# One fp32 transformer pair on one core: all riding modulation summed on VectorE, query statistics inside units, rstd spread by a broadcast stationary, and a slab's last tiles handled one by one

## The chip, the cores and the metric

The kernel runs on one core of one Trainium2 chip. The metric is the device time of one execution in microseconds (us). TensorE is PE here, VectorE DVE, ScalarE ACT, GpSimd POOL, and SyncE, which issues most of the transfers, SP.

## What is computed

Two transformer blocks run one after the other over 256 tokens of width 1024 (with 256 context tokens beside them in the first part). All matrices are fp32.

```python
# first block, S = 256 tokens, D = 1024
ml = split(silu(c) @ w_mod + b_mod, 9)            # the modulation: 9 chunks of 1024, for tokens and for context
x = x + 0.5 * ml[2] * swiglu(modulate(rms_norm(x), ml[0], ml[1]))    # "ffn1", inner width 2816; the context too
...                                                # w_in, 8 query heads, attention, convolution, gates, "merge", "wout"
x = x + 0.5 * ml[8] * swiglu(modulate(rms_norm(x), ml[6], ml[7]))    # "ffn2"
x = rms_norm(x, final_g)
# second block
h = rms_norm_2(x, norm_mix)                        # then its own attention, pooling and "wout2"
x = x + square(relu(rms_norm_2(x, norm_mlp) @ w_ff1)) @ w_ff2        # "ff", inner width 4096
return rms_norm_2(x, norm_final)
```

## The kernel before

All five engines run programs written by hand, tied by semaphores. Features lie on the 128 partitions and tokens in the columns, so an activation of width 1024 is 8 tiles (`KD`).

**Units.** The weights are cut into 161 units of 1 MB (eight 128-row blocks by 256 columns; some have six blocks). SP loads unit k into `raw[k % 2]`. ACT rounds it into `w_hi` (L510, `split`), in two halves; DVE takes the rest into `w_lo` (L945, its own `split`); PE multiplies in three products, high by high, low by high and high by low (L1702 to L1704; where both activations lie side by side, L1699 does the first two in one matmul of 512 columns). PE then adds to `halves_done`, the result is taken out of PSUM `ps_u`, and `drained` counts that. SP may load unit k + 2 once both halves of `w_lo` of unit k are made. Each engine's queue is in program order, so where a `split` stands decides what waits behind it.

**ffn1** is three slabs of inner tiles (8, 8 and 6 units), each followed by 4 output units (`out_step`), 34 units in all. Beside it ride the modulation's weights: 36 loads of 1 MB, a quarter of a chunk each. The first 8 (`MOD_FRONT`) are multiplied on PE before ffn1 (`front_mod`, L1662), with dummy matmuls between them (`keep_busy_front`, L1764). Of the other 28 (`MOD_RIDE`), 20 (`MOD_SUMMED`) are multiplied and summed on DVE during ffn1, four instructions a quarter (`mod_products`, L977 and L980), and after four quarters PE sums the partitions (`mod_sum`, L1678, 16 instructions in the trace) and DVE turns the chunk into columns (`modulation`, L989). The last 8 quarters go through PE (`late`, L1662): one in ffn1, seven around the norm behind it.

**A norm** between stages goes like this. DVE adds an output unit onto the pair of tiles of `x` (`add_out`, L1062). ACT squares both (`squares`, L555). POOL adds the squares of tiles 0 to 5 into tile 0 as they come. PE sums over partitions, 128 tokens a matmul of one column (`stat`, L1640: tiles 6, 7 and the sum). ACT takes the root (L539), DVE the reciprocal (L1010) and four diagonal matrices out of it (L1013, two for 256 tokens), PE multiplies these by ones, which spreads the value over the partitions (`spread`, L1646), and DVE scales each tile (L1024), ACT rounds it (L547), DVE makes the rest (L1033), and PE's next unit takes tile by tile. `keep_busy` (L1651) fills PE with dummy matmuls meanwhile.

**Queries** come as 4 units q0 to q3. Each head's squares are summed over partitions by `q_stat`, four matmuls a unit (L1834): three units' worth stand behind q3 and the fourth behind the first gates unit.

**ff** has four slabs of 4 inner units (8 tiles) and 4 output units. Of an inner unit ACT copies half of the result (L597), DVE adds the other half (L1070), takes relu and the row factor (L1604), ACT squares (L899) and rounds (L901), and DVE makes the rest (L1608), each time for both tiles of the unit in one instruction of 512 columns. The output unit needs tiles 6 and 7 last.

## Time and profile before

| what | value |
|---|---|
| median of 3 runs | 1279.79 us (1277.67, 1279.79 and 1280.79) |
| the profiled execution | 1281.16 us |
| its span, first to last instruction | 1279.4 us |
| PE busy | 1253.2 us, 98% |
| DVE busy | 850.3 us, 66% |
| ACT busy | 588.9 us, 46% |
| DMA | 214.22 MB, mean 167 GB/s |
| mean granted clock of PE | 0.993 |

The profiled execution took 1.76 us beyond its span and lay 1.37 us above the median. A time in the sections below is counted from the start of the span. One fp32 matmul shows as two records, so that 12 matmuls of `stat` are 24 records.

### The profile page before, as it was taken

To read this page: it belongs to the slowest core of one execution; us is meant where nothing else is said; L and a number is where in the kernel's file an instruction comes from. 1 tells how busy PE (TensorE), PEld (TensorE's weight loads), DVE (VectorE), ACT (ScalarE), POOL (GpSimd) and SP (SyncE) were. 2 spreads that over 40 slices of the span, in tenths; PEclk is the share of its full clock that TensorE was granted. 3 is DMA by queue.
4 is the path that set the end of the run, shared out by engine and by line. 5 is a ranking of instruction groups with operands and counts; after the bars stand their busy time and mean duration, and the time that the engine had idled before them with its cause. 6 is when DMAs were issued, how large, how long until landed. Compare 5 with 4: busy or idle time off the path is not lost.

```text
span 1279.4 us, 20913 instructions
## 1 busy us (share of the span) xinstructions
PE 1253.2 (98%) x7854; PEld 1097.3 (86%) x7854; DVE 850.3 (66%) x1356; ACT 588.9 (46%) x878; POOL 53.3 (4%) x65
## 2 busy tenths in 40 slices
PE   8999999999999999999999999999999999999997
PEld 6788888888887899888999888888899999888886
DVE  3677777763344755777666676666769977666765
ACT  3543234321233336644435654546465565554552
POOL 2000000000002000100001000000001301000001
PEclk8999999999999989999999999999999999999999
DMA  9655544444224334423445555554533334455442
GB/s 376 262 197 197 198 180 170 180 193 164 91 75 165 132 132 137 159 98 105 160 169 173 217 197 180 189 190 146 218 132 120 111 132 169 161 190 201 166 169 95
DMA packets 30962, 214.22 MB, mean 167 GB/s; under 512 B 3376, under 2 KB 4656, under 8 KB 5936
## 3 DMA queue, kind: packets, MB, share of 16 engines
q1 hardware_dynamic: 30320, 211.83, 45.9%
q10 hardware_dynamic: 576, 1.48, 0.3%
q8 instruction: 46, 0.75, 0.2%
q14 instruction: 20, 0.16, 0.0%
HBM read 212.24 MB, written 1.05 MB: 167 GB/s over the span
## 4 chain that ended last, share of the span: by engine, by line
PE 85%; DVE 6%; DMA 4%; ACT 3%; issue 1%; DVEq 0%; SPq 0%; ACTq 0%
PE ps_u L1704 25%; PE ps_u L1702 18%; PE ps_u L1703 18%; PE ps_u L1699 15%; DMA raw<-in_stream 2%; DVE w_lo L945 2%; PE ps_a L1628 1%; PE ps_a L1662 1%; PE ps_a L1881 1%; DMA wide_scr<-in_mods 1%; DMA scr<-in_mods 1%; PE ps_a L1866 1%; ACT w_hi L510 1%; PE ps_a L2065 1%; DVE sq L1024 1%
## 5 line engine op out<-in xcount | busy, mean ns | idle before, releaser
L945 DVE TENSOR_TENSOR w_lo<-raw,w_hi 128x1024 fp32r<-128x1024 f32 x322 | 393.4, 1224 | 148.4 <-ACT w_hi L510 147.3
L510 ACT ACTIVATE w_hi<-raw 128x1024 fp32r<-128x1024 f32 x322 | 339.1, 1056 | 323.2 <-PE ps_u L1704 222.5
L1704 PE MATMUL ps_u<-x_hi,w_lo 128*128 128x256 f32 (+1 forms) x1488 | 462.1, 311 | 0.0
L1702 PE MATMUL ps_u<-x_hi,w_hi 128*128 128x256 f32 (+1 forms) x1136 | 370.6, 326 | 2.2 <-DVE x_lo L1033 1.9
L1703 PE MATMUL ps_u<-x_lo,w_hi 128*128 128x256 f32 (+1 forms) x1072 | 345.2, 322 | 0.0
L1704 PEld LDWEIGHTS ps_u<-x_hi,w_lo 128*128 128x128 f32 x1488 | 283.8, 191 | 15.1
L1704 PE MATMUL ps_u<-h_hi,w_lo 128*128 128x256 f32 (+1 forms) x800 | 244.0, 305 | 0.0
L1702 PEld LDWEIGHTS ps_u<-x_hi,w_hi 128*128 128x128 f32 x1136 | 217.5, 191 | 21.1 <-issue 5.2
L1703 PEld LDWEIGHTS ps_u<-x_lo,w_hi 128*128 128x128 f32 x1072 | 205.3, 191 | 16.0 <-issue 0.7
L1704 PEld LDWEIGHTS ps_u<-h_hi,w_lo 128*128 128x128 f32 x800 | 151.6, 189 | 6.9
L1702 PE MATMUL ps_u<-h_hi,w_hi 128*128 128x256 f32 (+1 forms) x432 | 141.9, 328 | 0.8 <-DVE x L1062 0.4
L1699 PE MATMUL ps_u<-h_hi,w_hi 128*128 128x512 f32 x368 | 130.5, 399 | 3.2 <-DVE h_hi L1608 3.2
L1699 PE MATMUL ps_u<-x_hi,w_hi 128*128 128x512 f32 x352 | 125.0, 400 | 0.2 <-DVE x_hi L1033 0.2
L1703 PE MATMUL ps_u<-h_lo,w_hi 128*128 128x256 f32 (+1 forms) x368 | 122.9, 334 | 0.0
L1699 PE MATMUL ps_u<-x_lo,w_hi 128*128 128x512 f32 x256 | 90.4, 398 | 0.7 <-DVE h_hi L1608 0.7
L1702 PEld LDWEIGHTS ps_u<-h_hi,w_hi 128*128 128x128 f32 x432 | 82.1, 190 | 9.4 <-issue 1.2
L1699 PEld LDWEIGHTS ps_u<-h_hi,w_hi 128*128 128x128 f32 x368 | 69.1, 188 | 21.5 <-DVE h_hi L1608 3.9
L1699 PEld LDWEIGHTS ps_u<-x_hi,w_hi 128*128 128x128 f32 x352 | 66.1, 188 | 17.6 <-issue 0.8
L1703 PEld LDWEIGHTS ps_u<-h_lo,w_hi 128*128 128x128 f32 x368 | 69.9, 190 | 6.9
L1704 PE MATMUL ps_u<-x_lo,w_lo 128*128 128x256 f32 x256 | 71.5, 279 | 0.0
L1070 DVE TENSOR_TENSOR s<-ps_u,s 128x512 f32<-128x512 f32 x38 | 26.3, 692 | 52.8 <-ACT s L597 52.3
L1699 PEld LDWEIGHTS ps_u<-x_lo,w_hi 128*128 128x128 f32 x256 | 48.1, 188 | 12.4 <-DVE h_hi L1608 1.0
(277 smaller groups left out, 1215.6 us busy)
## 6 DMA issues: line engine op xcount, KB each, us to landing
raw<-in_stream SPq DMA_DIRECT2D x153, 1024.0 KB, 4.8
wide_scr<-in_mods SPq DMA_DIRECT2D x18, 1024.0 KB, 7.1
scr<-in_mods SPq DMA_DIRECT2D x18, 1024.0 KB, 6.9
raw<-in_stream SPq DMA_DIRECT2D x8, 768.0 KB, 4.2
x<-in_tokens SPq DMA_DIRECT2D x2, 1024.0 KB, 6.6
wide_scr<-in_cmp_w SPq DMA_DIRECT2D x2, 1024.0 KB, 7.8
sq<-in_cmp_w SPq DMA_DIRECT2D x2, 1024.0 KB, 7.5
out<-x SPq DMA_DIRECT2D x4, 256.0 KB, 2.2
```

The costliest lines, as they stand in the source:

```text
L510: act.activation(w_hi[:, k % 2, cols], raw[:, k % 2, cols], ACT.Copy).then_inc(h_ready, 1)
L945: dve.tensor_tensor(w_lo[:, k % 2, cols], raw[:, k % 2, cols], w_hi[:, k % 2, cols].bitcast(F32), ALU.subtract).then_inc(l_ready, 1)
L1024: ins = dve.scalar_tensor_tensor(sq[:, kc, cols], x[:, kc, cols], scale(kc, s), ps_a[:, 2, spread_cols], ALU.mult, ALU.mult)
L1070: dve.tensor_tensor(both, ps_u[:, b:b + 2, 0:S], both, ALU.add).then_inc(halves_summed, 1)
L1628: return pe.transpose(dst, src, ident[0:n, 0:n])
L1662: ins = pe.matmul(ps_a[rows, b, 0:MOD_COLS], sc_pad[:, 2 * quarter + kc, :], mod_slots[slot][:, lo:lo + MOD_COLS], start=(quarter == 0 and ...
L1699: pe.matmul(ps_u[:, 2 * b + t, :], wh, both, start=(kc == 0), stop=False)
L1702: pe.matmul(dst, wh, xh, start=(kc == 0), stop=False)
L1703: pe.matmul(dst, wh, xl, start=False, stop=False)
L1704: ins = pe.matmul(dst, wl, xh, start=False, stop=(kc == span - 1))
L1866: ins = pe.matmul(ps_a[:, qt, :], q_cur[:, j, qt * P:(qt + 1) * P], k_all[:, g, :], start=True, stop=True)
L1881: ins = pe.matmul(ps_a[:, 2, 0:S], v_tok[:, c, g, :], probs_t[:, c, :], start=(c == 0), stop=(c == 3))
```

## The change

The eight quarters that went through PE are multiplied on DVE as the twenty before them (`MOD_SUMMED` is 28), so all 28 riding loads are issued within ffn1, and PE gets two more `mod_sum`. What DVE and ACT did after ffn1 for the second block's gate weights (`wg_hi`, `wg_lo`) moves into it. `keep_busy_front` starts with 31 dummies instead of 22. `q_stat` is called within the units q2, q3 and the first two gates units. `spread` no longer takes diagonals: the stationary operand is the reciprocal itself, broadcast along the columns, and the identity is streamed, 128 columns a matmul. In three norms `stat` is cut into the sum's part and the part of tiles 6 and 7, with dummies between. A new semaphore, `first_added`, lets ACT start on the first tile of a pair. At the norms two halves of `split` move ahead of `add_out`, one behind `norm_lo`. And in ff the last inner unit of a slab goes tile by tile.

```diff
 MOD_RIDE = N_MOD * MOD_QUARTERS - MOD_FRONT
-MOD_SUMMED = 5 * MOD_QUARTERS
...
-MOD_BANKS = (0, 1, 2, 0, 1)
+MOD_BANKS = (0, 1, 2, 0, 1, 2, 0)
...
                     sp.wait_ge(mod_done, MOD_FRONT + n - 3)
-                elif n < MOD_SUMMED + 4:
+                else:
                     sp.wait_ge(mod_added, 4 * (n - 3))
-                else:
-                    sp.wait_ge(mod_done, MOD_FRONT + n - MOD_SUMMED - 3)
                 mod_load(MOD_FRONT + n, n % 4)
 
...
-                if n <= MOD_RIDE - 4:
-                    riding_load(n)
+                riding_load(n)
...
             units(FIRST["k"], 2)
-            for n in range(MOD_RIDE - 3, MOD_RIDE):
-                riding_load(n)
             run(FIRST["k"] + 2, FIRST["ffn2"])
...
+                    if t == 0 and early is not None:
+                        act.wait_ge(first_added, early)
+                    else:
+                        act.wait_ge(drained, 2 * pr + (k + 3))
                     act.activation(sq[:, m + t, 0:n], x[:, m + t, 0:n], ACT.Square).then_inc(sq_ready, 1)
...
                 if last and i == 3:
                     squares(pr, k0 + 2, 4, n)
-                    squares(pr, k0 + 3, 6, n)
+                    if more:
+                        split(pr, k0 + 5, 0)
+                    squares(pr, k0 + 3, 6, n, early)
...
                 dve.wait_ge(root_done, n + 1)
                 dve.reciprocal(rstd[:, 0:tiles], root[:, 0:tiles]).then_inc(recip_done, 1)
-                dve.wait_ge(recip_done, n + 1)
-                for t in range(tiles):
-                    ins = dve.tensor_scalar(t1[:, 0, t * P:(t + 1) * P], ident, rstd[:, t:t + 1], None, ALU.mult)
-                ins.then_inc(diag_done, 1)
...
+                    if first and t == 0:
+                        ins.then_inc(first_added, 1)
                 ins.then_inc(drained, 1)
...
                 hurry = last and more and i >= 2
-                if more and not (hurry and i == 3):
+                if hurry and i == 3:
+                    split(pr, k0 + i + 1, 1)
+                if more:
                     split(pr, k0 + i + 2, 0)
                 if made is not None:
                     add_halves(pr, k0 + i, 2 * i, gate, made + i)
                 else:
-                    add_out(pr, k0 + i, 2 * i, n, gate)
-                if hurry and i == 3:
-                    split(pr, k0 + i + 1, 1)
+                    add_out(pr, k0 + i, 2 * i, n, gate, first=last and i == 3)
                 if more and not hurry:
                     split(pr, k0 + i + 2, 1)
 
...
+
+            dve.memset(sq_gain[:, :, 0], 1.0)
+            dve.tensor_tensor(sq_gain[:, :, 1], vec[:, V_F1:V_F1 + KD], vec[:, V_F1:V_F1 + KD], ALU.mult)
...
+                                if c == 5:
+                                    scale_of(2, 7, V_N3)
+                                if c == 6:
+                                    gates_of(1, 8)
+                            if at + u == MOD_SUMMED:
+                                dve.wait_ge(wg_done, 1)
+                                dve.tensor_tensor(wg_lo[:], wg, wg_hi[:].bitcast(F32), ALU.subtract).then_inc(wg_ready, 1)
...
             swiglu(FIRST["ffn1"], 0, NB, 0)
-            dve.wait_ge(wg_done, 1)
-            dve.tensor_tensor(wg_lo[:], wg, wg_hi[:].bitcast(F32), ALU.subtract).then_inc(wg_ready, 1)
-            split(0, FIRST["k"] + 1, 0)
             spread(1, 4)
-            split(0, FIRST["k"] + 1, 1)
             dve.wait_ge(scale_ready, 2)
             norm_lo(1, 1, NB, modulated(1, 4), 3)
-            modulation(7, 7, 0)
-            scale_of(2, 7, V_N3)
-            modulation(8, 8, 1)
-            gates_of(1, 8)
+            split(0, FIRST["k"] + 1, 1)
...
-            split(0, FIRST["ffn2"] + 1, 0)
             spread(2, 2)
+            norm_lo(2, 2, S, modulated(2, 7), 6, beside=True)
             split(0, FIRST["ffn2"] + 1, 1)
-            norm_lo(2, 2, S, modulated(2, 7), 6, beside=True)
             swiglu(FIRST["ffn2"], 22, S, 1)
...
+                    if u < 3:
+                        two = slice(2 * u, 2 * u + 2)
                         dve.scalar_tensor_tensor(both, both, 0.0, r_both, ALU.max, ALU.mult).then_inc(relu_done, 1)
...
+                    else:
+                        for t in range(2):
+                            dve.scalar_tensor_tensor(both[:, t, :], both[:, t, :], 0.0, r_ff, ALU.max, ALU.mult).then_inc(relu_done, 1)
+                        split(pr, k + u + 2, 0)
+                        for t in range(2):
+                            m = 2 * u + t
+                            dve.wait_ge(hh_done, c + m - u + 1)
+                            ins = dve.tensor_tensor(h_hi[:, m, S:NB], t1[:, j, t * S:(t + 1) * S], h_hi[:, m, 0:S].bitcast(F32), ALU.subtract)
+                            ins.then_inc(drained if t else last_lo, 1)
+                    split(pr, k + u + 2, 1)
...
+            def stat(n, tiles):
+                stat_rows(n, tiles, (*range(SUMMED, KD), 0), SUMMED, 0)
+
+            def stat_sums(n, tiles):
+                stat_rows(n, tiles, (0,), 0, KD - 1)
+
+            def stat_rest(n, tiles):
+                stat_rows(n, tiles, range(SUMMED, KD), 0, KD - 1)
...
             def spread(n, tiles):
-                pe.wait_ge(diag_done, n + 1)
-                pe.matmul(ps_a[:, 2, 0:tiles * P], ones[:], t1[:, 0, 0:tiles * P], start=True, stop=True).then_inc(rb_done, 1)
+                pe.wait_ge(recip_done, n + 1)
+                for t in range(tiles):
+                    ins = pe.matmul(ps_a[:, 2, t * P:(t + 1) * P], rstd[:, t:t + 1].broadcast_to([P, P]), ident, start=True, stop=True)
+                ins.then_inc(rb_done, 1)
...
-            def late(n):
-                u = MOD_FRONT + n
-                c = u // MOD_QUARTERS
-                mod(u, 1 if c == N_MOD - 1 else 0, u % MOD_QUARTERS, n % 4, LANDED * (n // 4 + 3), c - 1)
...
                             c, behind = divmod(k + o - 1, MOD_QUARTERS)
                             if behind == MOD_QUARTERS - 1 and c < MOD_SUMMED // MOD_QUARTERS:
                                 mod_sum(c)
-                            if k + o == MOD_SUMMED + 2:
-                                late(MOD_SUMMED)
...
-            keep_busy_front(22)
+            keep_busy_front(31)
...
-            late_units = iter(range(MOD_SUMMED + 1, MOD_RIDE))
-            for n in itertools.islice(late_units, 3):
-                late(n)
-            stat(1, 4)
-            for n in itertools.islice(late_units, 2):
-                late(n)
+            pe.wait_ge(cst_landed, 16)
+            pe.wait_ge(mod_turned, N_MOD)
+            stat_sums(1, 4)
+            keep_busy(3)
+            stat_rest(1, 4)
+            keep_busy(2)
             spread(1, 4)
-            for n in late_units:
-                late(n)
+            keep_busy(4)
...
+            unit(0, kq + 3, from_x(S), ready=stat_within(1))
 
             pe.wait_ge(k_ready, 2)
...
-            gates(0, 0)
-            q_stat(3)
-            gates(0, 1)
+            gates(0, 0, stat_within(2))
+            gates(0, 1, stat_within(3))
...
-            keep_busy(3)
-            stat(2, 2)
+            stat_sums(2, 2)
+            keep_busy(2)
+            stat_rest(2, 2)
             keep_busy(2)
             spread(2, 2)
-            keep_busy(4)
+            keep_busy(3)
...
+            def hidden_ready(pr, k, slab):
+                def ready(kc):
+                    if kc == 6:
+                        pe.wait_ge(last_lo, slab + 1)
+                    else:
+                        pe.wait_ge(drained, 2 * pr + (k + kc // 2 + 3))
+                return ready
...
+            stat_sums(5, 2)
             keep_busy(2)
-            stat(5, 2)
+            stat_rest(5, 2)
             keep_busy(2)
             spread(5, 2)
```

PE where ffn1 ends, before: output units (L1704), late quarters (L1662), statistics (L1640), the spread (L1646), then the first unit of w_in.

```order
L1704 MATMUL ps_u<-h_hi,w_lo 128x512
L1662 MATMUL ps_a<-wide_scr,sc_pad 32x256 x8
L1662 MATMUL ps_a<-scr,sc_pad 32x256 x16
L1640 MATMUL ps_a<-ones,sq 128x1 x12
L1662 MATMUL ps_a<-wide_scr,sc_pad 32x256 x16
L1646 MATMUL ps_a<-t,ones 128x512
L1662 MATMUL ps_a<-scr,sc_pad 32x256 x16
```

The same place with the change (statistics L1658, spread L1675, dummies L1681):

```order
L1658 MATMUL ps_a<-ones,sq 128x1 x4
L1681 MATMUL ps_a<-cst,ones 128x256 x3
L1658 MATMUL ps_a<-ones,sq 128x1 x8
L1681 MATMUL ps_a<-cst,ones 128x256 x2
L1675 MATMUL ps_a<-cst,rstd 128x128 x4
L1681 MATMUL ps_a<-cst,ones 128x256 x4
```

The seven late quarters are gone, the sum's part of the statistics stands first, and dummies stand where the quarters stood.

DVE at the same place, before: the last addition (L1062), weight remainders (L945), gate weights (L1190), reciprocal, diagonals, and the first tiles of the norm.

```order
L1062 SCALAR_TENSOR_TENSOR x<-ps_u,gate_half,x 128x256 x8
L945 TENSOR_TENSOR w_lo<-raw,w_hi 128x1024
L1190 TENSOR_TENSOR wg_lo<-late_w,wg_hi 128x192
L945 TENSOR_TENSOR w_lo<-raw,w_hi 128x1024
L1010 RECIPROCAL rstd<-root 128x4
L1013 TENSOR_SCALAR t<-cst,rstd 128x128 x4
L945 TENSOR_TENSOR w_lo<-raw,w_hi 128x1024
L1024 SCALAR_TENSOR_TENSOR sq<-x,am,ps_a 128x256 x4
L1033 SCALAR_TENSOR_TENSOR x_lo<-sq,mods,x_hi 128x256 x2
```

With the change (L1066 is the addition, L955 the remainders, L1018 the reciprocal, L1028 and L1037 the norm):

```order
L1066 SCALAR_TENSOR_TENSOR x<-ps_u,gate_half,x 128x256 x4
L955 TENSOR_TENSOR w_lo<-raw,w_hi 128x1024 x2
L1066 SCALAR_TENSOR_TENSOR x<-ps_u,gate_half,x 128x256 x4
L1018 RECIPROCAL rstd<-root 128x4
L1028 SCALAR_TENSOR_TENSOR sq<-x,am,ps_a 128x256 x4
L1037 SCALAR_TENSOR_TENSOR x_lo<-sq,mods,x_hi 128x256 x2
```

Nothing stands any more between the last addition, the reciprocal and the norm.

DVE at the last inner unit of an ff slab, with the change; before, the row of L1621 was one instruction of 512 columns, and so was that of L1626.

```order
L1076 TENSOR_TENSOR s<-ps_u,s 128x512
L1621 SCALAR_TENSOR_TENSOR s<-s,q_cur 128x256 x2
L955 TENSOR_TENSOR w_lo<-raw,w_hi 128x1024
L1626 TENSOR_TENSOR h_hi<-t,h_hi 128x256 x2
L955 TENSOR_TENSOR w_lo<-raw,w_hi 128x1024 x2
```

The weight half stays between the relu and the remainder, as before.

## Rows read from the trace of the kernel before

**Rows 1.** The page's busy part: us (share of the span) xinstructions.

```profile
PE 1253.2 (98%) x7854; PEld 1097.3 (86%) x7854; DVE 850.3 (66%) x1356; ACT 588.9 (46%) x878; POOL 53.3 (4%) x65
```

**Rows 2.** Waits of PE: waiting line <- releaser: us in total, times, longest.

```profile
PE ps_u L1699 <- DVE h_hi L1608: 3.9, 6, 0.8
PE ps_a L1662 <- DMA wide_scr<-in_mods: 2.9, 1, 2.9
...
PE ps_a L1646 <- DVE t L1013: 1.4, 2, 0.7
...
PE ps_a L1932 <- DVE x_lo L1107: 0.4, 1, 0.4
```

**Rows 3.** Timeline of the front: start us, us, engine, line, tiles, [idle before].

```profile
24.54 1.16 PE L1764 MATMUL ps_u<-ones 128*128 128x128 f32 x8
...
25.58 6.36 DVE L1024 SCALAR_TENSOR_TENSOR sq<-x,am,ps_a 128x256 f32<-128x256 f32 x16
...
32.37 1.07 PE L1662 MATMUL ps_a<-scr,sc_pad 128*32 128x256 f32 x16 [0.41 <-DMA scr<-in_mods]
...
34.12 0.44 DVE L989 STREAM_TRANSPOSE turned<-ps_a 128x256 f32<-128x256 f32 x1
```

**Rows 4.** Two `mod_sum` on PE's timeline, four ffn1 units apart.

```profile
47.94 1.07 PE L1678 MATMUL ps_a<-sq,one_col 128*32 128x256 f32 x16
...
92.72 1.07 PE L1678 MATMUL ps_a<-sq,one_col 128*32 128x256 f32 x16
```

**Rows 5.** Groups by line and form: xcount | busy us, mean ns of one | idle before.

```profile
L980 DVE SCALAR_TENSOR_TENSOR sq<-scr,sc_pad,sq 128x1024 f32<-128x1024 f32 x40 | 48.7, 1278 | 0.0
...
L1145 DVE TENSOR_TENSOR h_hi<-t,h_hi 128x256 f32 x22 | 9.4, 425 | 14.7 <-ACT h_hi L627 14.7
```

**Rows 6.** Timeline where ffn1 ends.

```profile
405.07 1.66 DVE L1062 SCALAR_TENSOR_TENSOR x<-ps_u,gate_half,x 128x256 f32<-128x256 f32 x4 [6.50 <-PE ps_u L1704]
...
407.69 2.84 PE L1640 MATMUL ps_a<-ones,sq 128*128 128x1 f32 x24
...
411.08 0.87 DVE L1013 TENSOR_SCALAR t<-cst,rstd 128x128 f32<-128x128 f32 x4
...
413.71 1.65 DVE L1024 SCALAR_TENSOR_TENSOR sq<-x,am,ps_a 128x256 f32<-128x256 f32 x4 [0.63 <-PE ps_a L1646]
...
426.07 0.88 DVE L1033 SCALAR_TENSOR_TENSOR x_lo<-sq,mods,x_hi 128x256 fp32r<-128x256 f32 x2 [0.19 <-ACT x_hi L547]
```

**Rows 7.** Query statistics on PE's timeline.

```profile
468.14 3.08 PE L1834 MATMUL ps_a<-ones,scr 128*128 128x1 f32 x24
```

**Rows 8.** Windows: stretch, length, busy (x started) of PE, PEld, DVE, ACT, POOL; clock, DMA share, GB/s.

```profile
463.00:467.00 4.00, 4.00 (x36) 4.00 (x35) 3.80 (x8) 1.06 (x1) 0.00 (x0) 1.00 0.33 96
470.00:478.00 8.00, 8.00 (x43) 8.00 (x44) 2.10 (x3) 1.39 (x3) 0.00 (x0) 0.57 0.41 133
```

**Rows 9.** Timeline between wout and ffn2.

```profile
701.65 1.11 PE L1651 MATMUL ps_a<-cst,ones 128*128 128x256 f32 x4
703.47 0.70 PE L1646 MATMUL ps_a<-t,ones 128*128 128x256 f32 x2 [0.70 <-DVE t L1013]
...
704.46 0.86 DVE L1024 SCALAR_TENSOR_TENSOR sq<-x,am,ps_a 128x256 f32<-128x256 f32 x2
```

**Rows 10.** Timeline of the first ff slab's last inner unit, and PE's wait in the last slab.

```profile
1109.51 0.69 DVE L1604 SCALAR_TENSOR_TENSOR s<-s,q_cur 128x512 f32<-128x512 f32 x1
...
1111.88 0.69 DVE L1608 TENSOR_TENSOR h_hi<-t,h_hi 128x512 f32 x1 [0.54 <-ACT h_hi L901]
...
1112.63 0.49 PE L1699 MATMUL ps_u<-h_hi,w_hi 128*128 128x512 f32 x1 [0.68 <-DVE h_hi L1608]
...
1250.21 0.51 PE L1699 MATMUL ps_u<-h_hi,w_hi 128*128 128x512 f32 x1 [0.63 <-DVE h_hi L1608]
```

**Rows 11.** Timeline of the final norm.

```profile
1270.25 1.50 PE L1640 MATMUL ps_a<-ones,sq 128*128 128x1 f32 x12 [0.43 <-ACT sq L555]
...
1273.56 3.22 DVE L1621 SCALAR_TENSOR_TENSOR x<-x,vec,ps_a 128x256 f32<-128x256 f32 x8 [0.79 <-PE ps_a L1646]
```

More of the change, by code:

```diff
@@ L1051, in plain, with add_out @@
                 return lambda kc, s: vcol(v, kc)
-            def add_out(pr, k, m, n, gate, b=None):
+            def add_out(pr, k, m, n, gate, b=None, first=False):
                 done(pr, k)
@@ L1100, in out_parts @@
             def out_parts(n, k, m, gate, dst, hi, gain):
-                add_out(0, k, m, S, gate)
+                add_out(0, k, m, S, gate, first=True)
                 if m < KD - 2:
@@ L1628, in turn, with stat_rows @@
                 return pe.transpose(dst, src, ident[0:n, 0:n])
-            def stat(n, tiles):
+            def stat_rows(n, tiles, rows, first, last):
                 made = n if n < 3 else n - 1
-                for kc in (*range(SUMMED, KD), 0):
+                for kc in rows:
                     if kc == 0:
@@ L1812, in turn_v, with q_stat, stat_within @@
                 ins.then_inc(v_turned, 1)
+            def q_stat(i):
+                pe.wait_ge(q_squared, 2 * i + 2)
+                for h in range(2 * i, 2 * i + 2):
+                    for t in range(TT):
+                        at = 16 + TT * h + t
+                        ins = pe.matmul(ps_a[:, 1, at:at + 1], q_sq[:, h, t * P:(t + 1) * P], ones[:, 0:1], start=True, stop=True)
+                ins.then_inc(qstat_done, 1)
+            def stat_within(i):
+                return lambda kc: q_stat(i) if kc == 4 else None
             kq = FIRST["q"]
```

126 lines of the change are left out of this document (62 added, 64 removed).

## The prediction, written before the changed kernel ran

> **What bounds the kernel now.** I read the page first: PE is busy 98% of the span, so the time is PE's queue, and only two things can shorten it: work taken off PE, and stretches in which it idles, runs dummies, or runs at the low clock [rows 1]. Then PE's waits, to see who holds it: the three that this change touches are the remainder of the last ff tiles (3.9 us in six waits), the diagonals of the spread (1.4 in two) and one tile of `x_lo` (0.4) [rows 2]. Waits alone miss what dummies and late quarters cover, so I read the timeline at each norm, and last the windows, for the clock. There the reader sees a stretch behind the query statistics at a mean granted clock of 0.57.
>
> **Front.** PE waits 2.9 us for the first quarter [rows 2], and 31 dummies instead of 22 fill that. What ends the front is another chain: DVE scales tiles from 25.58 for 6.36 us, makes two weight halves (2.35 us) and turns the second chunk at 34.12, while PE waited for the last quarter's load until 32.37 and then multiplied for 1.07, to 33.44 [rows 3]. The loads don't come sooner for a faster PE, as they queue behind each other. So at most 34.12 - 33.44 = 0.7 us is to be had, if DVE's scaling starts sooner (no diagonals, a warm PE). The spread by four matmuls of 128 columns costs 1.16 us (eight records [rows 3]). I take **0.6 us gained**, bounds 0 and 0.7.
>
> **ffn1.** PE loses one late quarter and gets two `mod_sum`, 1.07 us each, as each quarter is also 1.07 [rows 3, 4]. Net **1.1 us lost**. DVE gets 8 quarters of four instructions at 1.28 us, about 5.1 us a unit [rows 5]. Two sums are 44.8 us apart, that is four units of 10.9 and the sum [rows 4]; DVE's other work in such a unit (two weight halves of some 1.2 us, two products or four additions, 1.66 [rows 6]) leaves about 2 us of it free, as it did for the 20 units before, in which PE has no wait for DVE [rows 2]. So DVE's share costs nothing; without that slack it would cost PE up to 5 us a unit.
>
> **Where ffn1 ends.** PE's last output unit is over at about 405.0 (DVE adds from 405.07). Before, three quarters run first, the statistics take 407.69 to 410.5, 24 records of 0.116 us, then quarters, the diagonals from 411.08 for 0.87, and the scaling starts at 413.71, 3.25 us behind the statistics [rows 6]. With the change: the sum's part, 8 records, 0.93 us, to 405.9; three dummies, six records at some 0.25 (four take 1.11 [rows 9]), 1.5 us, to 407.4; tiles 6 and 7, 16 records, 1.86 us, to 409.3, whose squares are there by then (added by 406.73 [rows 6]). Two dummies, 1.1 us, cover root and reciprocal; the spread takes 1.16 and DVE starts some 0.2 later: 411.7. That is **2.0 us gained**, as the first w_in unit goes at the norm's pace to its last tile, at 426.95 before [rows 6]. The half `split` that now stands behind the norm is needed only halfway through the next unit; the next load waits on it and comes later than before, two units ahead of its use. The transposes that followed the norm are gone, but PE had the next unit's weights. Unknown is the broadcast stationary operand: no row shows one. From below it costs nothing more than the dummies' load. From above I let each of eight weight loads stand uncovered for 0.1 us, 0.8 in all. I take the low end, as dummies whose operand changes nothing in kind run at 0.145 a record [rows 3]. Bounds 1.2 and 2.4.
>
> **Query statistics.** 24 records take 3.08 us behind q3 [rows 7]. In the 8 us from 470 the clock granted is 0.57 of full, the lower of its two levels (1.2 GHz) for most of it, and 43 matmuls start; at the full clock (2.4 GHz) 36 start in 4 us [rows 8]. 43 would take 4.8 us: 3.2 us are lost. What PE did before the fall is that string of matmuls of one column. With the change no more than 8 records stand together. The matmuls themselves stay. I take **3.0 us gained**, bounds 0 and 3.4 (half of 8 x 0.86).
>
> The Trainium skill bears on that (TensorE: Matmul & The Clock Gate, Part 1): the gate halves the clock by how busy PE has lately been, it does not start afresh with a kernel, so where it falls varies from run to run. The trace has the fall at this place, in full. By the rule some runs of before may not have the fall at all, and then the sum gains nothing here; that is a rival below.
>
> **Between wout and ffn2.** The dummies behind the statistics start at 701.65, the scaling at 704.46, 2.8 us later, with PE's wait of 0.70 for the diagonals and a weight half in DVE's queue between [rows 9]. With the change two dummies (1.1), two spread matmuls (0.6, half of 1.16) and 0.2: 1.9, so 0.9 gained. The sum's part, 4 records or 0.45 us, goes ahead. **1.3 us gained**, bounds 0.7 and 1.6. The load that a moved half releases comes later, and the two loads of compression weights with it; the one is two units ahead of its use, the others are for the second block.
>
> **Into the second block.** The wait of 0.7 for the diagonals (half of 1.4) and that of 0.4 for `x_lo` go [rows 2]: the reciprocal is there when PE is, and ACT rounds tile 6 while DVE adds tile 7, one addition earlier (0.4, a quarter of 1.66 [rows 6]). **1.1 us gained**, bounds 0.4 and 1.1.
>
> **ff.** In each of four slabs PE waits at tile 6 of the first output unit, from 0.68 in the first to 0.63 in the last; the sum over the four is 2.6 of the 3.9 [rows 2, 10] (two other waits, in the first slab, stay: they hang on units that the change leaves whole). The relu starts at 1109.51, the remainder of both tiles at 1111.88 and PE at 1112.63 [rows 10]. One by one: an instruction of 256 columns takes 0.425 against 0.69 [rows 5, 10], so both relus end some 0.1 later than one did, the weight half behind them too (0.6 from start to start for the relu, 0.1 more, 1.2 for the half), at about 1111.45. ACT has by then squared and rounded tile 6. Its remainder then ends at 1111.9, and PE starts at 1112.0, when it is ready anyway (1112.63 - 0.68 = 1111.95). 0.6 of each wait goes, and no more than the wait: **2.4 us gained**, bounds 1.0 and 2.6. Tile 7 follows 0.4 later, under PE's matmuls of tile 6.
>
> The skill has a rule against this step (VectorE: DVE Perf Modes, The TRN2 errata): each instruction pays a fixed latency, so tiles of at least 512 elements are the better ones. The rows bear the rule out: 2 x 0.425 is 0.16 more than 0.69 [rows 5, 10]. By the rule DVE and ACT lose a little in each slab; by the rows the first tile still comes sooner, and neither engine ends the slab.
>
> **End.** The statistics shrink by the sum's 0.45 us, while root, dummies and spread take 1.9 as before (from about 1271.7 to 1273.56 [rows 11]). **0.4 us gained**, bounds 0.2 and 0.9.
>
> **Sum.** 0.6 - 1.1 + 2.0 + 3.0 + 1.3 + 1.1 + 2.4 + 0.4 = 9.7 us. Against the profiled execution of 1281.16 us that is 1271.5. It lies 1.37 above the median of before, 1279.79, from which the sum gives 1270.1. Either could be the better base, as the runs spread by 3.5 us; I take **1270.8 us**.
>
> **Rivals.**
> *The clock falls elsewhere, or fell in few runs before* (0.20). For it: the runs shown spread from 1277.67 to 1280.79, about the size of one fall. Against: the profiled run has it in full. Then 6.7 us are gained, 1273.1 from the median, or 1274.5 from the profile.
> *The slabs of ff keep their wait* (0.08): ACT's queue is what is late, as its weight half stands ahead of the copy. Without the 2.4: 1273.2.
> *More is gained* (0.05): the front is freed more than the loads seem to allow, by the 2.9 us of the first wait, 1268.
> *DVE falls behind in ffn1* (0.04). This one ends on the other side. In the 8 units that newly carry quarters a weight half would come late and PE wait. For it: 5.1 us more a unit. Against: 20 units of the same kind show none. It decides from 1.7 us a unit on: 8 x 1.7 = 13.6 us, time 1284.7.
> *The gain is given back* (0.05): each norm starts sooner and the next unit waits for its weights or loads instead, so that only q and ff remain at half size: 1277.
> The forecast has 0.58, and its own range is 1268 to 1273.5.
>
> A measurement of this kernel tells about 0.3%, 3.8 us, from no change, so faster means under 1276.0. Forecast, clock, ff and the larger gain lie there, 0.91, of which I give 0.03 to the zone between for bounds that add up badly: faster 0.88, same 0.08, slower 0.04. The range reaches from all upper bounds that are likely together, 1267, to past the clock rival, 1276: it leaves out about 2 in 10.
>
> **What the profile after would show.** No low clock around 470, and the same number of q statistics in four pieces. Statistics where ffn1 ends over at about 4.3 us behind the last unit, scaling at 6.7 (8.7 before). No wait for L1013, which is gone. The waits of L1699 for the remainder at about 1.3 us in total instead of 3.9. Two sums more in ffn1, and no PE wait on DVE there. The prediction is wrong if the clock falls at another place, if the broadcast operand makes a spread matmul longer than 0.3 us, or if waits on weight halves appear behind the norms.

## The result, and the profile after

The changed kernel took 1265.93 us, the median of four runs (1263.96 to 1267.28), against 1278.73 for the kernel before in runs on the same chip (four, 1276.84 to 1280.79): a ratio of 0.9894, 95% interval 0.9873 to 0.9915. The profiled run took 1267.28, its span 1265.5. Between the two profiled spans lie 13.9 us; I had worked out 9.7, and the time of 1265.9 is under my range of 1267 to 1276. Taken a second time, among the experiments, it had 1265.84 us (0.9892, 0.9866 to 0.9917).

The page's busy part and span, with the columns of [rows 1]:

```profile
span 1265.5 us, 20715 instructions
...
PE 1247.6 (99%) x7814; PEld 1098.2 (87%) x7814; DVE 883.0 (70%) x1378; ACT 589.2 (47%) x886; POOL 54.5 (4%) x65
```

PE's busy time fell by only 5.6 us where the span fell by 13.9: most of the gain is waits. PE's waits, as [rows 2] shows them for before:

```profile
PE ps_a L1692 <- DMA scr<-in_mods: 2.2, 1, 2.2
PE ps_u L1727 <- DVE x_lo L1037: 1.9, 2, 1.3
PE ps_a L2087 <- DVE q_cur L1519: 1.7, 2, 1.1
...
PE ps_u L1724 <- DVE h_hi L1154: 0.7, 1, 0.7
```

The top row of before, six waits of 3.9 us for the remainder of the ff tiles, has gone altogether (I had left 1.3 of it), and so have the diagonals. One row of those shown is new, the last: 0.7 us of wait in ffn2.

To see where the 13.9 us lie I cut both profiled executions at the same PE instructions (times between the starts of these, in us):

| stage, ended by | before | after | gained | forecast |
|---|---|---|---|---|
| front, first `mod_sum` | 47.94 | 48.45 | -0.5 | +0.6 |
| ffn1 and its norm, key statistics | 391.94 | 390.19 | +1.8 | -1.1 + 2.0 |
| k, v, q units, first swap of the gates | 39.72 | 36.68 | +3.0 | +3.0 |
| attention, wout, behind wout's last unit | 219.11 | 219.09 | 0.0 | 0 |
| norm, first unit of ffn2 | 7.43 | 5.40 | +2.0 | +1.3 |
| ffn2 | 190.79 | 190.41 | +0.4 | 0 |
| norm, first stage of the second block | 18.92 | 17.34 | +1.6 | +1.1 |
| second block, statistics ahead of ff | 171.55 | 171.55 | 0.0 | 0 |
| ff | 181.40 | 176.86 | +4.5 | +2.4 |
| final norm, end of the span | 10.59 | 9.53 | +1.1 | +0.4 |

The largest miss is ff, 2.1 us of the 4.2 by which the sum was short. The table compares one profile of each kernel. Some stages of the old code vary between its profiles: ff took 180.3 to 184.1 us in five of them (176.9 to 177.5 in three of the new), the stage into the second block 18.6 to 18.9 in seven (17.3 in all of the new).

In the first slab's last inner unit of after, what answers to [rows 10] reads, in order of time, with one row of ACT (it squares the two tiles) among those of DVE:

```profile
1099.01 0.68 DVE L1076 TENSOR_TENSOR s<-ps_u,s 128x512 f32<-128x512 f32 x1
1099.72 0.76 DVE L1621 SCALAR_TENSOR_TENSOR s<-s,q_cur 128x256 f32<-128x256 f32 x2
...
1100.18 0.76 ACT L909 ACTIVATE t<-s 128x256 f32<-128x256 f32 x2 [0.33 <-DVE s L1621]
1100.40 1.22 DVE L955 TENSOR_TENSOR w_lo<-raw,w_hi 128x1024 fp32r<-128x1024 f32 x1
...
1101.54 0.75 DVE L1626 TENSOR_TENSOR h_hi<-t,h_hi 128x256 fp32r<-128x256 f32 x2
```

From the start of the relu to the start of the first remainder it takes 1.8 us; before it took 1109.51 to 1111.88, 2.4. PE multiplies all the while.

Where ffn1 ends, against [rows 6]:

```profile
406.65 0.94 PE L1658 MATMUL ps_a<-ones,sq 128*128 128x1 f32 x8
...
408.84 1.84 PE L1658 MATMUL ps_a<-ones,sq 128*128 128x1 f32 x16
...
411.01 0.18 DVE L1018 RECIPROCAL rstd<-root 128x4 f32<-128x4 f32 x1 [2.50 <-ACT root L535]
...
411.49 1.05 PE L1675 MATMUL ps_a<-cst,rstd 128*128 128x128 f32 x8
...
412.65 1.66 DVE L1028 SCALAR_TENSOR_TENSOR sq<-x,am,ps_a 128x256 f32<-128x256 f32 x4 [1.46 <-PE ps_a L1675]
```

The scaling starts 6.0 us behind PE's last output unit; 8.7 before, 6.7 forecast. The broadcast operand costs nothing: 8 records in 1.05 us, where 8 of a dummy with the same 128 columns took 1.16 [rows 3].

The clock at the query statistics, and in the front (windows as in [rows 8]):

```profile
457.00:479.00 22.00, 22.00 (x185) 21.79 (x183) 12.99 (x20) 9.40 (x14) 0.00 (x0) 1.00 0.39 139
```

```profile
32.00:36.00 4.00, 3.37 (x24) 2.10 (x25) 1.91 (x4) 0.68 (x2) 0.00 (x0) 0.57 0.69 223
```

The fall near 470 is gone (1.00 throughout), but in the front there is one at 32 to 36, a granted clock of 0.57, on the very chain that ends the front.

### The profile page after: what moved, and what is told of

It reads as the page before. It is cut to its first block, busy times and chain, and to the rows that moved or that the text cites. A ratio compares the mean times of both kernels' runs of the same rounds, so it can differ in the third digit from the quotient of the medians.

```text
span 1265.5 us, 20715 instructions
## 1 busy us (share of the span) xinstructions
PE 1247.6 (99%) x7814; PEld 1098.2 (87%) x7814; DVE 883.0 (70%) x1378; ACT 589.2 (47%) x886; POOL 54.5 (4%) x65
## 3 DMA queue, kind: packets, MB, share of 16 engines
HBM read 212.24 MB, written 1.05 MB: 169 GB/s over the span
## 4 chain that ended last, share of the span: by engine, by line
PE 92%; DVE 3%; DMA 2%; ACT 1%; issue 1%; SPq 0%; DVEq 0%; ACTq 0%
PE ps_u L1729 27%; PE ps_u L1727 19%; PE ps_u L1728 19%; PE ps_u L1724 17%; PE ps_a L1646 1%; DMA wide_scr<-in_mods 1%; DVE w_lo L955 1%; PE ps_a L1902 1%; DMA scr<-in_mods 1%; PE ps_a L1887 1%; PE ps_a L1658 1%; PE ps_a L1703 1%; PE ps_a L2087 1%; DMA raw<-in_stream 1%; PE ps_a L1681 0%
## 5 line engine op out<-in xcount | busy, mean ns | idle before, releaser
L955 DVE TENSOR_TENSOR w_lo<-raw,w_hi 128x1024 fp32r<-128x1024 f32 x322 | 393.3, 1223 | 120.0 <-ACT w_hi L506 119.0
L1728 PEld LDWEIGHTS ps_u<-x_lo,w_hi 128*128 128x128 f32 x1072 | 204.0, 190 | 15.5 <-issue 0.5
L988 DVE SCALAR_TENSOR_TENSOR sq<-scr,sc_pad,sq 128x1024 f32<-128x1024 f32 x56 | 68.1, 1279 | 0.0
```

The source lines that it names most:

```text
L955: dve.tensor_tensor(w_lo[:, k % 2, cols], raw[:, k % 2, cols], w_hi[:, k % 2, cols].bitcast(F32), ALU.subtract).then_inc(l_ready, 1)
L988: ins = dve.scalar_tensor_tensor(total_v, w[:, kc, :], by, total_v, ALU.mult, ALU.add)
L1728: pe.matmul(dst, wh, xl, start=False, stop=False)
```

## Experiments

In the tables, **time beyond pace** is summed over PE's matmuls of one stage: what each start-to-start distance has over 237 ns (512 columns) or 120 ns (256), where it is over by more than 15%.

### The inner units of ff written out, the tiles still in pairs

The diff also turned the `Fori` loop over the inner units, which computes its addresses in registers, into straight code; I had priced only the tiles that go singly. This kernel is the one before with this alone, on ACT and DVE:

```diff
-                with dve.Fori(0, 2) as p:
-                    for j in range(2):
-                        sum_halves(k + j, j, c - 22 + 2 * p + (j + 1))
+                for u in range(4):
+                    j = u % 2
+                    sum_halves(k + u, j, c - 22 + u + 1)
...
-                        two = ds(4 * p + 2 * j, 2)
+                    two = slice(2 * u, 2 * u + 2)
```

> The kernel before with one edit: the inner units of an ff slab are written out one by one on ACT and DVE instead of in a loop of two over register addresses; both tiles of the last one stay together. In the two traces that I have, the ff stage took 178.4 us before and 173.8 after, 4.7 less where I had forecast 2.4. Theory U (the loop's address work was part of each wait): the six waits for the remainder (3.9 us) shrink to under 1.5, the stage takes about 175.7 us (2.7 less: 0.34 from each of four chains and the 1.3 of the first slab), the time is about 1276, ratio 0.998. Theory T (the tiles going singly did it all): the stage stays at 178.4 within 0.4, the time at that of before.

1274.94 us (12 runs) against 1278.76: ratio 0.9971, 0.9956 to 0.9986, that is 3.7 us. The stage ff took 178.51, the waits that were 3.9 us are off the list of PE's waits. Its neighbour, the changed kernel with the last inner unit's tiles in a pair again:

```diff
-                    if u < 3:
+                    if u < 4:
...
-                    if kc == 6:
-                        pe.wait_ge(last_lo, slab + 1)
-                    else:
-                        pe.wait_ge(drained, 2 * pr + (k + kc // 2 + 3))
+                    pe.wait_ge(drained, 2 * pr + (k + kc // 2 + 3))
```

> The changed kernel with one part undone: the last inner unit of a slab is rounded, squared and left with its remainder as a pair of tiles again; the loops stay written out. Theory U: about 0.3 us of wait comes back in each slab but no more, the ff stage takes 175 to 176 us, the time is 1267.5 to 1268.5. Theory T: all waits are back, the stage takes 178.4, the time is 1270.6.

1267.17 us (0.9900, 0.9882 to 0.9918), the stage 178.09. The expectations count ff from the start of its second unit, 3.0 us behind the table's cut; by the table's, theory U expected 178.7 and 178 to 179, and theory T 181.4 for both. U holds; the 3.7 us in the runs are more than the 2.7 that it gave.

### Which engine's loop

The same edit on one engine each, in the kernel before.

> The kernel before with one edit: DVE's inner units of an ff slab are written out, ACT's stay in the loop over register addresses (both tiles of the last one together). PE's time beyond its pace in ff was 4.8, 5.8 and 8.1 us in kernels with both loops and 2.0 with both written out. If DVE's loop is what made the remainder late (theory D), it falls to under 3 here; if ACT's (theory A), it stays over 4; if each adds its share of the address work, both this kernel and its counterpart show 3 to 4. Time by D: 1275.5, by A: 1278 or more.

> The counterpart: ACT's inner units of an ff slab are written out, DVE's stay in the loop. Theory D: PE's time beyond its pace in ff stays over 4 us, the time at 1278 or more. Theory A: it falls to under 3 us, the time to 1275.5. Shares: 3 to 4 us in both.

| kernel | loops on | beyond pace in ff | stage ff | ratio to before |
|---|---|---|---|---|
| before, two profiles | both | 5.8, 5.5 | 181.4, 180.3 | 1 |
| three other kernels with that code | both | 4.8, 8.1, 4.8 | 180.4, 184.1, 181.3 | |
| ACT written out | DVE | 4.3 | 178.9 | 1.0012 (1.0001 to 1.0024) |
| DVE written out | ACT | 2.9 | 178.4 | 0.9982 (0.9965 to 1.0000) |
| both written out | none | 2.0 | 178.5 | 0.9971 (0.9956 to 0.9986) |
| changed, tiles in a pair | none | 1.4 | 178.1 | 0.9900 (0.9882 to 0.9918) |
| changed, two profiles | none | 0.9, 0.6 | 176.9, 177.4 | 0.9894, 0.9892 |

From the start of the relu to the start of the remainder (all 16 units) it takes 2.30 to 2.39 us before, 2.20 to 2.29 with ACT written out, 2.15 to 2.17 with DVE and 2.06 with both; in the changed kernel the first of two single tiles makes it 1.82. The remainder's group, by line and form, tells it directly. Its last figure is DVE's idle time ahead of these 16 instructions. In order: before taken a second time, DVE written out, ACT written out, both:

```profile
L1608 DVE TENSOR_TENSOR h_hi<-t,h_hi 128x512 f32 x16 | 11.1, 692 | 8.7 <-ACT h_hi L901 8.7
```

```profile
L1608 DVE TENSOR_TENSOR h_hi<-t,h_hi 128x512 fp32r<-128x512 f32 x16 | 11.1, 692 | 5.3 <-ACT h_hi L901 5.3
```

```profile
L1608 DVE TENSOR_TENSOR h_hi<-t,h_hi 128x512 f32 x16 | 11.1, 692 | 7.0 <-ACT h_hi L901 7.0
```

```profile
L1608 DVE TENSOR_TENSOR h_hi<-t,h_hi 128x512 fp32r<-128x512 f32 x16 | 11.1, 693 | 3.7 <-ACT h_hi L901 3.7
```

The instruction itself is as long in all four. What shrinks is the pause ahead of it, by 3.4 us through DVE's loop and 1.7 through ACT's (of 8.7): 0.21 and 0.11 us a unit, or 0.3 of a chain that was 0.5 to 0.9 us too long. Most is DVE's, as theory D had it, and the shares of the pause add up. ACT's own share stands in its rows too, as idle time for which the view names no releaser, ahead of the instruction that makes `h_hi`: 2.2 us with the loop (before taken a second time), 0.5 without (ACT written out).

```profile
L901 ACT ACTIVATE h_hi<-t 128x512 f32 x16 | 10.1, 632 | 2.2
```

```profile
L901 ACT ACTIVATE h_hi<-t 128x512 fp32r<-128x512 f32 x16 | 10.1, 633 | 0.5
```

The times add up less well than the pauses: 2.3 us gained by DVE's loop alone (1277.18 us, where theory D expected 1275.5), 3.7 by both, and by ACT's alone no gain, if anything a loss of 1.5 us that no stage of its profile shows (its profiled run was its quickest, 1274.92, with the quick pace in ffn2 of which the last section tells). That PE's wait fell by more than the chain's 0.3 us a slab, and to nothing, is seen but not fully explained: with both loops, single waits in a slab ran from 0.2 to 2.3 us between executions, and what made the long ones stays open.

### The query statistics within units

```diff
+            def stat_within(i):
+                return lambda kc: q_stat(i) if kc == 4 else None
...
-            unit(0, kq + 3, from_x(S))
-            for i in range(3):
-                q_stat(i)
+            unit(0, kq + 3, from_x(S), ready=stat_within(1))
```

> The kernel before with one edit: the query statistics go into units, eight matmuls at a time. Theory C (the string of 24 matmuls of one column is what the clock falls behind): no low clock near 470, the q stage 3.0 us shorter, the time 1275.7. Rival: the fall comes from what was run earlier and only moves; then the low clock stands somewhere within the next 20 us and the time stays within 1 us of before.

1276.76 us (0.9976, 0.9960 to 0.9991). The stage of the query units took 36.68 us against 39.72 and the clock stayed up there, but where ffn1 ends a fall came that the first profile of before didn't have, and cost 1.3 us (393.23 against 391.94):

```profile
409.00:413.00 4.00, 4.00 (x41) 2.98 (x44) 3.02 (x7) 1.63 (x3) 0.00 (x0) 0.75 1.01 424
413.00:417.00 4.00, 4.00 (x46) 1.45 (x38) 1.89 (x5) 0.58 (x2) 0.00 (x0) 0.82 1.02 426
464.00:478.00 14.00, 14.00 (x118) 13.90 (x117) 9.46 (x15) 6.48 (x9) 0.00 (x0) 1.00 0.37 121
```

So was the string of one-column matmuls the cause, or did the fall only move? I broke the string with dummies:

```diff
             for i in range(3):
+                if i:
+                    for _ in range(2):
+                        pe.matmul(ps_a[:, 1, S:2 * S], ones[:], cos1, start=True, stop=True)
                 q_stat(i)
```

> The kernel before with one edit: between the three groups of eight query statistics behind q3 stand two dummies of 256 columns each, 1.0 us a time, 2.0 in all. In all three profiles of kernels with the plain string of 24 the clock falls within 3 us of its start, for 3.4 or 6.8 us, and in none of the three without. Theory C (a long stretch of one-column matmuls is behind the fall): no low clock from 465 to 480, and the q stage takes 36.7 + 2.0 = 38.7 us. Rival (something else ahead of it is behind the fall, such as the whole load since 440): the clock falls all the same and the stage takes 40.2 to 41.7.

No low clock there, and a stage of 38.42 us (the 24 records of statistics in three pieces and 2 us of dummies, full clock), where 38.7 was expected:

```profile
469.00:480.00 11.00, 11.00 (x88) 10.79 (x88) 4.30 (x6) 3.95 (x5) 0.00 (x0) 1.00 0.37 136
```

And the kernel before again:

> The kernel before as it is, a second time, for where its clock falls. Of the five profiles so far with its code where ffn1 ends, three have the fall in the string of query statistics near 470 and none near 411, and the two without that string have one near 411. If a fall comes at one of the two places in each run (theory O), this profile shows exactly one of them, at 411 or at 470. If the two are independent, it may show both or none; the fall at 470 is then expected in any case.

```profile
409.00:413.00 4.00, 4.00 (x40) 2.40 (x39) 2.90 (x7) 1.21 (x2) 0.00 (x0) 0.57 0.99 393
...
470.00:478.00 8.00, 8.00 (x44) 8.00 (x44) 2.10 (x3) 1.24 (x2) 0.00 (x0) 0.57 0.40 131
```

Both places in one execution: theory O falls. So the fall where ffn1 ends in the kernel with the query statistics moved was not the one from 470, moved: the kernel before has it there too. Over all profiles: the plain string of 24 records has the fall behind it in six of six, for 3.4 us (four) or 6.8 (two), and the stage then takes 38.2 or 39.7 us; where it is split and no dummies stand in it, 36.68 in seven of seven. The old code where ffn1 ends has a fall in five of eight, 1.3 us each; the new one, as changed, in none of four.

### The broadcast spread alone

```diff
-                pe.matmul(ps_a[:, 2, 0:tiles * P], ones[:], t1[:, 0, 0:tiles * P], start=True, stop=True).then_inc(rb_done, 1)
+                for t in range(tiles):
+                    ins = pe.matmul(ps_a[:, 2, t * P:(t + 1) * P], rstd[:, t:t + 1].broadcast_to([P, P]), ident, start=True, stop=True)
+                ins.then_inc(rb_done, 1)
```

> The kernel before with one edit: the rstd is spread by matmuls with a broadcast operand as the weights, and DVE makes no diagonals. If the broadcast operand costs nothing more than a dummy's, the two waits for diagonals (1.4 us) go and 0.5 us more where ffn1 ends: 1.5 to 2.2 us faster, 1276.6 to 1277.3. If its weights load slowly, the spread records are longer than 0.3 us each and the gain is under 1 us.

1277.20 us (0.9989, 0.9971 to 1.0008): the runs don't settle it. The stages tell more: ahead of the second block 17.34 us instead of 18.92, all of that stage's gain; at the end 10.23 instead of 10.59; between wout and ffn2 only 7.18 instead of 7.43, where I had given the spread 0.9. Where ffn1 ends it shows nothing: the stage took 391.62, and 391.94 and 391.60 with the old spread and no fall of the clock. Between wout and ffn2 DVE was the one behind:

```profile
699.71 1.23 DVE L944 TENSOR_TENSOR w_lo<-raw,w_hi 128x1024 fp32r<-128x1024 f32 x1 [0.67 <-ACT w_hi L509]
...
700.85 0.16 DVE L1009 RECIPROCAL rstd<-root 128x2 f32<-128x2 f32 x1
...
701.18 1.23 DVE L944 TENSOR_TENSOR w_lo<-raw,w_hi 128x1024 fp32r<-128x1024 f32 x1 [0.17 <-ACT w_hi L509]
```

One weight half holds the reciprocal, the next the scaling, which starts at 702.33.

### The two weight halves back ahead of that norm

```diff
-            spread(2, 2)
-            norm_lo(2, 2, S, modulated(2, 7), 6, beside=True)
-            split(0, FIRST["ffn2"] + 1, 1)
+            split(0, FIRST["ffn2"] + 1, 0)
+            spread(2, 2)
+            split(0, FIRST["ffn2"] + 1, 1)
+            norm_lo(2, 2, S, modulated(2, 7), 6, beside=True)
```

> The changed kernel with one part undone: on DVE, the two weight halves at the norm between wout and ffn2 stand again as before, one ahead of the reciprocal and one ahead of the scaling. From the start of that stage's statistics to the first w_in matmul it takes 7.4 us before, 7.2 with the broadcast operand alone, 5.4 with the whole change. Theory H (the halves in DVE's queue were the wait): 0.9 to 1.3 us comes back, 6.3 to 6.7. Theory S (the split statistics and the earlier square did it): at most 0.3 comes back, 5.4 to 5.7.

The norm took 6.36 us, as theory H had it: the half ahead of the scaling is worth 0.96 us there. The half ahead of the reciprocal cost nothing any more, as the reciprocal starts 2.59 us behind the first statistics in both kernels. The 0.8 us between 7.18 and 6.36 came with the rest of the change at this norm (the statistics in two parts, the earlier square and weight halves on ACT, fewer dummies), which no run takes apart. But ffn2 took 189.48 instead of 190.41, and both together 195.84 against 195.81: the half behind the norm gives nothing. SP's queue in the changed kernel and in this one:

```profile
706.92 0.81 SPq L406 DMA_DIRECT2D wide_scr<-in_cmp_w  x2
712.29 12.90 SPq L364 DMA_DIRECT2D raw<-in_stream  x3
```

```profile
690.39 8.33 SPq L364 DMA_DIRECT2D raw<-in_stream  x2
698.93 0.81 SPq L406 DMA_DIRECT2D wide_scr<-in_cmp_w  x2
```

The load that the half behind the norm releases stands in SP's queue ahead of the two compression weights: counted from the statistics they go 12.5 us behind, not 5.5, and the next unit's weights, issued at 712.3 in both, wait behind them. ACT gets these at 718.74, in the kernel with the halves back at 717.02. ACT's copy of the result out of PSUM, and what DVE makes of it, stand behind that in their queues, and PE waits for them at 723 us, in the fifth unit of ffn2:

```profile
718.74 1.06 ACT L506 ACTIVATE w_hi<-raw 128x1024 fp32r<-128x1024 f32 x1 [3.26 <-DMA raw<-in_stream]
...
723.78 0.47 PE L1724 MATMUL ps_u<-x_hi,w_hi 128*128 128x512 f32 x1 [0.70 <-DVE h_hi L1154]
```

### The changed kernel again, and two tuned versions

> The changed kernel as it is, a second time, to be compared with the next ones on one chip and stage by stage. In the profiles so far the wide units of ffn2 and ff run at one of two paces, a pair of 512 and 256 columns in 347 or in 353 ns, and change between them at PE's waits. If that is what spreads the runs, this profile's stages without wide units (up to ffn2, and from the second block to ff) agree with the first one's within 0.1 us except for the front, and ffn2 and ff differ by up to 3 us. The time: 1264 to 1268.

All stages but the front and ff repeat within 0.02 us, ffn2 too. The front doesn't: no fall of the clock at 32, although PE idled longer there, and the first sum at 47.43 instead of 48.45:

```profile
32.48 1.07 PE L1692 MATMUL ps_a<-scr,sc_pad 128*32 128x256 f32 x16 [2.79 <-DMA scr<-in_mods]
...
33.62 0.45 DVE L997 STREAM_TRANSPOSE turned<-ps_a 128x256 f32<-128x256 f32 x1
```

The tuned kernel (the changed one, and):

```diff
-            keep_busy(3)
+            keep_busy(2)
             stat_rest(1, 4)
-            keep_busy(2)
+            keep_busy(1)
...
-                keep_busy_front(4)
+                keep_busy_front(16 if u == MOD_FRONT - 1 else 4)
...
-            run(FIRST["ffn2"], FIRST["ffn2"] + 4)
+            run(FIRST["ffn2"], FIRST["ffn2"] + 6)
             sp.wait_ge(drained, FIRST["wout"] + 2)
             cmp_weights(0)
```

with 2 and 2 dummies made 1 and 1 at the other two norms as well.

> The changed kernel with three edits: at the three norms that end with dummies one dummy less in each group (PE began the spread 0.3 us behind the reciprocal, and the last tiles' statistics up to 0.4 us behind the squares), the compression weights two loads later (a wait of 0.7 to 0.8 us in ffn2 goes), and 16 instead of 4 dummies ahead of the last front quarter, so that PE does not idle 2.2 us there. If each is worth what the rows show: 1.2 us at the norms, 0.8 in ffn2, and 0.9 in the front where the clock else falls: 1263.5, between 1262 and 1265. Rival: PE then waits for the squares and reciprocals instead, and the clock falls in the front all the same, so the time is that of the changed kernel within 1 us.

1263.14 us (0.9871, 0.9850 to 0.9893), on the same chip as the second 1265.84. The norms gave 0.4, 0.2 and 0.2 us, 0.8 of the 1.2; in ffn2 the wait moved two units on and became 0.4; the front gained nothing. The time is the one expected, 1263.5, but these rows make only some 1.1 of the 2.7 us. The same with 12 dummies in the front:

> The tuned kernel with 12 instead of 16 dummies ahead of the last front quarter. With 16 they ended at 33.0 us in the profile where the load had landed at 32.5, so the second chunk was turned at 34.2 and not at 33.6 as in the second profile of the changed kernel. If that is all, the first sum stands at 47.4 here (47.96 with 16), the other stages outside the wide units repeat within 0.1 us (396.4 from the sum to the end of the query stage's landmark less the front, 5.2 at the norm behind wout, 9.3 at the end), and the time is 1262.6, between 1260.5 and 1264. If the clock falls in the front all the same, 1263.6.

1266.19 us (1261.63 to 1266.91; 0.9876, 0.9854 to 0.9898), above the 1260.5 to 1264 that were expected, and a ratio within the changed kernel's interval. The front did as expected (first sum at 47.35; the expectation's 396.4 should read 426.4). But where ffn1 ends the clock fell, for 6.8 us, in the code with fewer dummies, which took 391.10 instead of 389.76:

```profile
405.00:409.00 4.00, 4.00 (x30) 3.56 (x29) 2.14 (x5) 1.26 (x2) 0.00 (x0) 0.98 0.00 0
409.00:416.00 7.00, 7.00 (x23) 5.93 (x24) 3.50 (x10) 2.91 (x6) 0.00 (x0) 0.53 0.00 0
```

So neither is shown to beat the changed kernel: the intervals of all three overlap, and the profile of the first, 1260.8 us, had the quick pace that the last section tells of.

## Why the prediction was right in its direction and too small

**ff, 2.4 forecast, 4.5 measured.** This is the step that failed. I wrote that "two other waits, in the first slab, stay: they hang on units that the change leaves whole", and that no more than 0.6 of each other wait would go "and no more than the wait", by single tiles. Those units stay whole but not unchanged: the diff takes them out of a loop. Written out alone, with pairs, the loops give 3.7 us in the runs; single tiles add 0.4 to 0.8 of time beyond pace (1.35 against 0.93 and 0.60). I had named the wrong cause for most of a right effect, and the upper bound of 2.6 stood on it. The loops' share was a term that the sum did not have at all. The 4.5 itself is of one pair of profiles; the means of all with the old code and with the new differ by 4.2. Two short relus take 0.76 us together, one long one 0.69. The Trainium skill's rule on short tiles (VectorE: DVE Perf Modes, The TRN2 errata) agrees in sign, at 0.07 us where I had allowed 0.16, and decides nothing here.

**Query statistics, 3.0.** Right in mechanism and size against this profile, and shown: the string broken in two ways, no fall. Not each run gives back 3.0: the fall is worth 1.5 or 3.0. My rival that it fell in few runs is not borne out (six of six profiles). Its other half, that the clock falls elsewhere, has a place I hadn't looked at, where ffn1 ends, but the kernel before has that fall as well. The Trainium skill says that the gate does not start afresh with a kernel, so that where the clock changes varies from run to run (TensorE: Matmul & The Clock Gate, Part 1). The place where ffn1 ends agrees: of the two profiles of before one has the fall there. Behind the long string it came each time.

**Where ffn1 ends, 2.0.** Mis-sized, not wrong. ffn1's own 1.1 us lost came as said (the last output unit ends at 406.65), with no wait of PE for DVE in it: the side on which the kernel would have been slower had nothing for it. The norm gave 2.9. I took merged rows' lengths as PE's time: a row of four dummies shows 1.11 us, but the next matmul starts 0.95 behind its start (410.54 to 411.49), since a row reaches to the end of its last matmul. Over the four rows ahead of the spread that is 0.55, and the 0.2 that I added behind the spread lies within its row: 6.0 and not 6.7. And before's own cost there varies by 1.3 with the clock. Which part of the change made the 2.9 was not taken apart there; the broadcast spread alone shows none of it.

**Wout to ffn2, 1.3.** 2.0 came, and 0.4 in ffn2. The spread, which I gave 0.9, is worth 0.25 by itself, 0.8 came with the statistics in two parts, ACT's earlier work and fewer dummies together, and 0.96 with the weight half that no longer stands ahead of the scaling. That last part is paid back in ffn2. I had priced the later load at nothing ("two units ahead of its use"); with the compression weights in front of the next one it cost 0.9. What offset it in ffn2 were two waits of 0.4 at its end, for DVE's last additions. Seven of eight profiles with the old code have them and none of the six with the new; I had not put them in the sum, and which part of the change removes them is not shown.

**Into the second block, 1.1, and the end, 0.4.** 1.6 and 1.1. The spread alone makes the first (1.2 to 1.6, by which profile of the old code is taken), so the 0.4 that I gave to ACT's earlier rounding had no part in it. At the end 0.36 is the spread. The other 0.7 I put down, without a run of its own, to the statistics' order and the earlier square, which I counted as the sum's 0.45 alone; PE's wait of 0.43 for that square [rows 11] is gone:

```profile
1255.96 0.50 PE L1658 MATMUL ps_a<-ones,sq 128*128 128x1 f32 x4
...
1257.28 0.95 PE L1658 MATMUL ps_a<-ones,sq 128*128 128x1 f32 x8
...
1259.68 3.22 DVE L1639 SCALAR_TENSOR_TENSOR x<-x,vec,ps_a 128x256 f32<-128x256 f32 x8 [0.96 <-PE ps_a L1675]
```

**Front, 0.6.** Not borne out. The first sum stands at 47.4 to 47.7 in three profiles of the new front and, after a fall of the clock, at 48.45 in the fourth; in six of the old one it stands at 47.1 to 48.3, 47.7 in the mean (and at 51.1 once, the kernel with ff written out, where the clock was low for 6.8 us from 19.4 and for 3.4 from 39.9). DVE scales 1.5 us sooner (from 24.07), but then it is PE's last quarter that is late, and that stands where its load lands:

```profile
32.63 1.93 PE L1692 MATMUL ps_a<-scr,sc_pad 128*32 128x256 f32 x16 [2.17 <-DMA scr<-in_mods]
```

At the full clock that row is 1.07 long.

**The bounds and the signs.** All my upper bounds together, with the 1.1 lost in ffn1, make 11.6 us. Between the profiles lie 13.9, so the bounds were too low and not only the middles: 2.6 for ff, 1.6 behind wout, 1.1 into the second block, 0.9 at the end. By its own chances the range left out hardly more than 1 in 10, not 2, and the rival in which DVE falls behind adds up to 1284.4, not 1284.7. Two signs of being wrong that I had named did show: the clock fell at another place (the front, in one of two profiles), and a wait on weights appeared behind a norm (0.7 us in ffn2). Neither is why the time is lower than forecast; both cost time.

## What to carry to other kernels

Read a diff for what it does to the instruction stream, not only to the work: a loop over register addresses was written out here, and the step from one engine's result to the other's next instruction became 0.3 us shorter a unit, with every instruction as long as before. When a norm's chain is late, look at what else stands in the queue of the engine that must answer first, and when something is moved out of it, follow the loads it released up to the next one that is short of time. Where matmuls of one column stand in a long string, look at the clock behind it; here the queries' strings of 8 records between wide matmuls had none behind them in eight profiles, and the string of 24 had one in six of six. Judge a change of one microsecond by stages cut at the same instruction in several profiles, not by one total.

## What the runs showed that I had not expected

**Two paces of the same matmuls.** In units that pair 512 with 256 columns, at a granted clock of 1.00 and with PE busy throughout, a pair takes 353 ns in most stretches and 347 in others. The same 100 us of ffn2, 740 to 840, in before and in the kernel with the spread alone (PE's count is in its brackets):

```profile
740.00:840.00 100.00, 100.00 (x568) 86.77 (x567) 68.83 (x98) 50.91 (x70) 0.00 (x0) 1.00 0.54 189
```

```profile
740.00:840.00 100.00, 100.00 (x579) 88.18 (x578) 70.34 (x102) 50.16 (x67) 0.00 (x0) 1.00 0.56 198
```

ffn2 took 187.6 to 187.9 us in the three profiles with the quick pace and 189.5 to 190.8 in the others, whatever the edit. A pace holds for tens of units, and most changes of it come with a wait of PE. Over ffn2 and ff, some 960 pairs, it is worth up to 6 us, more than most edits here, and may be much of why runs of one kernel differ by 3 to 9 us; that is argued from single profiles, and what sets the pace stays open, as no experiment was aimed at it.

**How long PE idled did not tell whether the clock fell.** In the changed kernel's front PE idled 2.17 us once and the clock fell; in the second profile it idled 2.79, in that of its neighbour with pairs 3.19, and the clock held. At the query statistics and where ffn1 ends it fell with PE counted as 100% busy, inside strings of 24 one-column records or up to 1.3 us behind their end.
